# Expert loop of a two-layer mixture model: down products ahead of the next gate and up, and the pair's sum in two parts

## The chip, the cores and the metric

The kernel runs on one core of one Trainium2 chip. The metric is the device time of one execution in microseconds. Times of the program before come from three runs; the profile is one more execution, recorded by the hardware profiler.

## The reference

A block of two layers on 256 tokens of width 1024, all in float32. Layer 0 mixes tokens by attention, layer 1 by pooled means. After each mixer every token goes to two of 32 experts (inner width 512):

```python
h2 = modulate(rms_norm(x, norm2_g[i]), sh2, s2)
experts, gates = route(h2, router_w, router_b)        # two experts and two gates for each token
...
def expert_block(args):
    xb, e = args
    return (jax.nn.silu(xb @ w_gate[e]) * (xb @ w_up[e])) @ w_down[e]
...
x = x + g2 * out                                      # out: gated sum over a token's two experts
```

## The kernel before

Five engine programs are written by hand and meet at counting semaphores; there is no scheduler. What matters here is `experts(L)`, which each of the engines has once for layer `L`, and the loads on SP.

*Tokens into slots.* Every expert has 64 slots. The tokens are gathered into `dense` (columns by slot) by products with a selection matrix on TensorE, in two halves of 256 slots; each half has eight steps k (L814, L819), and ScalarE and VectorE evict them with the modulation (L1180, L1749). GpSimd copies the 64 slots of expert e into one of two buffers `xw` (L465).

*One expert.* TensorE computes gate and up in two halves of four steps k each (`gate_up`, L825, 16 profiled matmul records a half) into PSUM bank 4. ScalarE applies silu (L1205), VectorE multiplies by up (L1773) and counts `h_ready`. TensorE transposes the hidden values (two, L835) into bank 5, ScalarE copies them to `t_sb` (L1199) and counts `t_ready`. TensorE computes the down product into bank 6 (`down`, L844) and counts `dn_done`. VectorE multiplies it by the layer's output gate into `y_sb`, in two column halves f (`gated_outputs`, L1755), and counts `y_v`, two for each expert.

*Two experts make a pair*, with 128 rows in `y_sb`. The pair's selection `sg` (VectorE's `choose`, L1740 and L1744) is transposed too (L833), and `combine` (L853) adds the rows back to the tokens in PSUM banks 0 to 3: two products for each half f. In the loop, e is the expert and c its place in a body of six; the second expert of a pair has c odd. Before the loop TensorE has done expert 0 whole and gate and up of expert 1.

*Weights.* The ring has three slots of one expert each. SP loads expert e in its queue's order: gate and up of the first half (2 DMAs of 1 MB) when TensorE has counted `gu_half` for expert e - 3, of the second half when it has counted `gu_done`, and down (2 MB) when it has counted `dn_done`. The landings are counted by `gu_in`, `gu2_in` and `dn_in`. Experts 0, 1 and 2 are loaded ahead of the layer's loop. Behind expert 31 of layer 0 the same queue loads the pool mixer's weights.

## Time and profile before

| | |
|---|---|
| three runs | 1310.32, 1314.6, 1315.19 us; median 1314.6 |
| profiled execution | 1308.68 us, span 1306.9 us |
| TensorE busy | 1200.5 us, 92% of the span |
| VectorE, ScalarE, GpSimd busy | 458.7, 178.4, 73.4 us |
| HBM read | 484.00 MB, 371 GB/s over the span |
| TensorE's granted clock | 0.982 of full speed |

The expert loops take some two thirds of the span: about 314 to 756 us for layer 0 and 860 to 1302 us for layer 1. A busy share is a mean over stages: which resource ends a stage last must be read inside it. In the rows further down PE is TensorE, ACT ScalarE, DVE VectorE, POOL GpSimd, and SPq a DMA issue on SP's queue.

### The profile page before, as it was taken

To read this page: it belongs to the slowest core of one execution; us is meant where nothing else is said; L and a number is where in the kernel's file an instruction comes from. 1 tells how busy PE (TensorE), PEld (TensorE's weight loads), DVE (VectorE), ACT (ScalarE), POOL (GpSimd) and SP (SyncE) were. 2 spreads that over 40 slices of the span, in tenths; PEclk is the share of its full clock that TensorE was granted. 3 is DMA by queue.
4 is the path that set the end of the run, shared out by engine and by line. 5 is a ranking of instruction groups with operands and counts; after the bars stand their busy time and mean duration, and the time that the engine had idled before them with its cause. 6 is when DMAs were issued, how large, how long until landed. Compare 5 with 4: busy or idle time off the path is not lost.

```text
span 1306.9 us, 13664 instructions
## 1 busy us (share of the span) xinstructions
PE 1200.5 (92%) x5008; PEld 492.8 (38%) x5008; DVE 458.7 (35%) x933; ACT 178.4 (14%) x375; POOL 73.4 (6%) x86
## 2 busy tenths in 40 slices
PE   6999999889999999898998899899999998988897
PEld 3444445544333333232332376443333332322232
DVE  4296676577122212121121156642222221211112
ACT  2212126522000000000000021310000000000000
POOL 0113100000000000000000000000000000000000
PEclk9999999999999999899998999999999998999999
DMA  9948759286999999999999997589999999999995
GB/s 355 399 184 347 261 205 401 97 346 251 410 422 421 422 423 422 421 422 422 422 422 423 418 406 297 222 329 415 422 422 422 422 421 422 422 422 422 422 422 235
DMA packets 80933, 485.50 MB, mean 371 GB/s; under 512 B 6146, under 2 KB 7682, under 8 KB 31748
## 3 DMA queue, kind: packets, MB, share of 16 engines
q1 hardware_dynamic: 79168, 481.91, 90.3%
q10 hardware_dynamic: 1732, 3.16, 0.7%
q8 instruction: 20, 0.33, 0.1%
q14 instruction: 13, 0.11, 0.0%
HBM read 484.00 MB, written 1.05 MB: 371 GB/s over the span
## 4 chain that ended last, share of the span: by engine, by line
PE 57%; SPq 18%; DMA 15%; DVE 4%; issue 3%; ACT 3%; POOL 0%; DVEq 0%; ACTq 0%
PE PS L825 19%; SPq L325 14%; DMA ring<-in_moe_w_up 13%; PE PS L844 10%; PE PS L635 8%; PE PS L853 4%; SPq L330 3%; PE PS L605 2%; PE PS L707 2%; PE PS L997 2%; PE PS L972 2%; DMA ring<-in_attn_w_in 2%; PE PS L835 1%; DVE KQH L1773 1%; ACT ring L1071 1%
## 5 line engine op out<-in xcount | busy, mean ns | idle before, releaser
L825 PE MATMUL PS<-ring,KQH 128*64 128x512 f32 x2048 | 480.5, 613 | 30.1 <-DMA ring<-in_moe_w_up 28.6
L825 PEld LDWEIGHTS PS<-ring,KQH 128*64 128x64 f32 x2048 | 146.1, 141 | 311.0 <-issue 277.0
L844 PE MATMUL PS<-ring,KQH 128*64 128x512 f32 x1024 | 230.8, 592 | 2.3 <-ACT KQH L1191 1.4
L844 PEld LDWEIGHTS PS<-ring,KQH 128*64 128x64 f32 x1024 | 73.0, 137 | 147.8 <-issue 144.6
L1755 DVE TENSOR_TENSOR TMP<-PS,KQH 64x512 f32<-64x512 f32 x64 | 44.1, 689 | 228.8 <-PE PS L844 227.8
L1755 DVE TENSOR_TENSOR TMP<-PS,TMP 64x512 f32<-64x512 f32 x64 | 44.1, 689 | 227.8 <-PE PS L844 226.7
L853 PE MATMUL PS<-TMP,KQH 128*128 128x512 f32 x256 | 118.4, 605 | 1.6 <-DVE TMP L1755 1.6
L1205 ACT ACTIVATE KQH<-PS 128x256 f32<-128x256 f32 x62 | 23.8, 384 | 665.5 <-PE PS L825 646.0
L635 PE MATMUL PS<-ring,KQH 128*128 128x512 f32 x256 | 114.0, 593 | 0.0
L1773 DVE TENSOR_TENSOR KQH<-KQH,PS 128x256 f32<-128x256 f32 x64 | 38.7, 605 | 157.3 <-ACT KQH L1205 157.3
L465 POOL COPY KQH<-KQH 128x512 f32 x62 | 38.1, 617 | 831.5 <-PE PS L825 771.2
L853 PEld LDWEIGHTS PS<-TMP,KQH 128*128 128x128 f32 x256 | 46.0, 189 | 73.6 <-issue 70.3
L635 PEld LDWEIGHTS PS<-ring,KQH 128*128 128x128 f32 x256 | 46.5, 190 | 54.0 <-issue 54.0
L1740 DVE TENSOR_SCALAR rope_g<-const,route 128x128 f32<-128x128 f32 x128 | 35.7, 342 | 76.1 <-PE PS L835 75.7
L835 PE MATMUL PS<-const,KQH 128*128 128x128 f32 x128 | 26.2, 287 | 34.0 <-DVE KQH L1773 34.0
L448 POOL TENSOR_TENSOR stat<-stat,mhalf 128x16 f32<-128x16 f32 (+3 forms) x18 | 35.0, 1942 | 361.3 <-DVE stat L1546 130.8
L1366 DVE SCALAR_TENSOR_TENSOR ring<-ring,ccols 128x1024 f32<-128x1024 f32 x42 | 54.0, 1285 | 3.3 <-DMA ring<-in_ada_w 1.8
L1199 ACT COPY KQH<-PS 128x256 f32<-128x256 f32 (+1 forms) x62 | 29.5, 476 | 147.4 <-PE PS L835 147.4
L835 PEld LDWEIGHTS PS<-const,KQH 128*128 128x128 f32 x128 | 14.4, 140 | 61.4 <-DVE KQH L1773 61.4
L605 PE MATMUL PS<-ring,KQH 128*128 128x512 f32 x64 | 29.4, 619 | 1.8 <-DMA ring<-in_attn_w_in 1.8
L707 PE MATMUL PS<-ring,KQH 128*128 128x512 f32 x64 | 28.0, 594 | 0.9 <-ACT KQH L1078 0.9
L972 PE MATMUL PS<-KQH,ring 128*128 128x257 f32 x128 | 28.2, 379 | 0.0
(249 smaller groups left out, 788.0 us busy)
## 6 DMA issues: line engine op xcount, KB each, us to landing
ring<-in_moe_w_gate SPq DMA_DIRECT2D x128, 1024.0 KB, 26.5
ring<-in_moe_w_up SPq DMA_DIRECT2D x128, 1024.0 KB, 26.6
ring<-in_moe_w_down SPq DMA_DIRECT2D x64, 2048.0 KB, 27.9
ring<-in_ada_w SPq DMA_DIRECT2D x23, 2048.0 KB, 13.3
ring<-in_attn_w_in SPq DMA_DIRECT2D x2, 4096.0 KB, 12.7
ring<-in_attn_w_in SPq DMA_DIRECT2D x2, 2048.0 KB, 21.0
ring<-in_attn_w_out SPq DMA_DIRECT2D x1, 4096.0 KB, 24.1
ring<-in_pool_w_in SPq DMA_DIRECT2D x1, 4096.0 KB, 27.9
```

Source lines behind the costliest of these rows:

```text
L325: sp.dma_start(gu_w[s][:, a, 4 * part:4 * part + 4, :], w[L.l, e].rearrange("(p k) f -> p k f", p=P)[:, 4 * part:4 * part + 4, :]).then_in ...
L605: ins = mm(bank(4 + 2 * n + half), hT[:, k, P * n:P * n + P], unit(2)[:, k, 512 * half:512 * half + 512], start=k == 0, stop=k == KC - 1)
L635: ins = mm(bank(4 + 2 * (n % 2) + half), hT[:, k, P * t:P * t + P], unit(u)[:, k, 512 * half:512 * half + 512], start=k == 0, stop=k == KC ...
L707: ins = mm(bank(4 + q), oT[:, h, P * (q // 2):P * (q // 2) + P], unit(2)[:, h, 512 * (q % 2):512 * (q % 2) + 512], start=h == 0, stop=h == ...
L825: ins = mm(PS[64 * f:64 * f + 64, 4, :], xs[:, k, 0:SLOTS], gu_w[s][:, :, k, 256 * f:256 * f + 256], start=k == 0, stop=k == KC - 1)
L835: ins = tr(PS[:, 5, 256 + P * c:256 + P * c + P], h_sb[:, P * c:P * c + P], ident)
L844: ins = mm(PS[64 * f:64 * f + 64, 6, :], lhs, dn_w[s][:, c, 512 * f:512 * f + 512], start=c == 0, stop=c == 3)
L853: ins = mm(bank(2 * t + f), t_sb[:, P * t:P * t + P], y_sb[:, 512 * f:512 * f + 512], start=False, stop=done is not None, skip_group_check ...
L972: ins = mm(PS[:, n % 4, 0:SEQ + 1], pool_w[:, k, P * b:P * b + P], xa[:, k, :], start=k == 0, stop=k == KC - 1)
L1366: ins = V.scalar_tensor_tensor(acc, unit(u)[:, k, :], ccols[:, 32 * k:32 * k + 1], acc, ALU.mult, ALU.add)
L1755: return V.tensor_tensor(y_sb[64 * second:64 * second + 64, 512 * f:512 * f + 512], PS[64 * f:64 * f + 64, 6, :], g[64 * f:64 * f + 64, 51 ...
L1773: V.tensor_tensor(h_pairs, silu_sb.rearrange("p (q b) -> p q b", b=2), PS[:, 4, 256:512].rearrange("p (q b) -> p q b", b=2), ALU.mult).the ...
```

## The change

It reorders TensorE's program and adapts ScalarE and VectorE to it.

- TensorE does, for each expert, transposes, down product, then gate and up of the next expert, both halves in a row. Before, down stood between the two halves.
- The sum of a pair (experts e - 1 and e, c odd) is split: its first column half comes behind gate and up of expert e + 1, the second behind gate and up of expert e + 2. Between them lie transposes and down of e + 1.
- The selection is transposed with the pair's second expert (c odd), before with its first.
- VectorE writes the second gated half of a pair's first expert only when TensorE has done the transposes of the next expert (`tr_done`), since the sum before reads these columns until then.
- At the layer's start, expert 0's transposes of the hidden values move between the gathers of k = 3 and 4 of the second half, with a copy of 256 columns instead of 512. The selection's transposes leave this place.
- The last pair of a layer is summed at once, as before.

```diff
--- before.py
+++ after.py
@@ -845,15 +845,55 @@
                                  start=c == 0, stop=c == 3)
                 return ins
 
-            def combine(L, y, done=None):
-
-                for f in range(2):
-                    pe.wait_ge(L.y_v, y + f + 1)
-                    for t in range(NT):
-                        ins = mm(bank(2 * t + f), t_sb[:, P * t:P * t + P], y_sb[:, 512 * f:512 * f + 512], start=False,
-                                 stop=done is not None, skip_group_check=True)
-                        if done is not None:
-                            ins.then_inc(done, 1)
+            def combine(L, y, f, done=None):
+
+                pe.wait_ge(L.y_v, y + f + 1)
+                for t in range(NT):
+                    ins = mm(bank(2 * t + f), t_sb[:, P * t:P * t + P], y_sb[:, 512 * f:512 * f + 512], start=False,
+                             stop=done is not None, skip_group_check=True)
+                    if done is not None:
+                        ins.then_inc(done, 1)
+
+            def second_places(L, k):
+
+                for t in range(NT):
+                    gather_high(1, k, t)
+                    ins = gather_low(1, k, t)
+                ins.then_inc(L.xg_done, 1)
+
+            def turn_hidden(L, e, c, it):
+
+                pe.wait_ge(L.h_ready, e + 1)
+                if c % 2:
+                    pe.wait_ge(L.sg_ready, 3 * it + (c // 2 + 1))
+                transposes(sg if c % 2 else None).then_inc(L.tr_done, 1)
+
+            def gate_up_first(L, e, c, it):
+
+                pe.wait_ge(L.gu_in[L.slot(c)], (2 * it + c // 3) * 32 + 32)
+                pe.wait_ge(L.xw_ready, e)
+                gate_up(L.slot(c), xw[c % 2], range(4)).then_inc(L.gu_half, 1)
+
+            def gate_up_second(L, e, c, it):
+
+                pe.wait_ge(L.gu2_in[L.slot(c)], (2 * it + c // 3) * 32 + 32)
+                gate_up(L.slot(c), xw[c % 2], range(4, KC)).then_inc(L.gu_done, 1)
+
+            def down_product(L, e, c, it):
+
+                pe.wait_ge(L.t_ready, e + 1)
+                pe.wait_ge(L.dn_in[L.slot(c)], (2 * it + c // 3) * 16 + 16)
+                pe.wait_ge(L.y_v, 2 * e)
+                down(L.slot(c)).then_inc(L.dn_done, 1)
+
+            def sum_and_next(L, e, c, it):
+
+                combine(L, 2 * e, 0)
+                turn_hidden(L, e + 1, c + 1, it)
+                down_product(L, e + 1, c + 1, it)
+                gate_up_first(L, e + 2, c + 2, it)
+                gate_up_second(L, e + 2, c + 2, it)
+                combine(L, 2 * e, 1)
 
             def combine_overflow():
 
@@ -887,57 +927,41 @@
                 pe.wait_ge(L.gu2_in[L.slot(0)], 32)
                 gate_up(L.slot(0), dense, range(4, KC)).then_inc(L.gu_done, 1)
                 pe.wait_ge(L.picked, 4)
-                for k in range(KC):
+                for k in range(4):
                     if k == 3:
                         pe.wait_ge(L.slots_known, 1)
-                    if k >= 4:
-                        pe.wait_ge((L.xs_v, L.xs_a)[k % 2], 4 + (k - 4) // 2 + 1)
-                    for t in range(NT):
-                        gather_high(1, k, t)
-                        ins = gather_low(1, k, t)
-                    ins.then_inc(L.xg_done, 1)
+                    second_places(L, k)
                 pe.wait_ge(L.h_ready, 1)
-                pe.wait_ge(L.sg_ready, 1)
-                transposes(sg).then_inc(L.tr_done, 1)
+                transposes(None).then_inc(L.tr_done, 1)
+                for k in range(4, KC):
+                    pe.wait_ge((L.xs_v, L.xs_a)[k % 2], k // 2 + 3)
+                    second_places(L, k)
                 pe.wait_ge(L.t_ready, 1)
                 pe.wait_ge(L.xs_v, 7)
                 pe.wait_ge(L.dn_in[L.slot(0)], 16)
                 down(L.slot(0)).then_inc(L.dn_done, 1)
-                pe.wait_ge(L.gu_in[L.slot(1)], 32)
-                pe.wait_ge(L.xw_ready, 1)
-                gate_up(L.slot(1), xw[1], range(4)).then_inc(L.gu_half, 1)
-                pe.wait_ge(L.gu2_in[L.slot(1)], 32)
-                gate_up(L.slot(1), xw[1], range(4, KC)).then_inc(L.gu_done, 1)
+                gate_up_first(L, 1, 1, 0)
+                gate_up_second(L, 1, 1, 0)
                 pe.wait_ge(L.xs_a, 8)
                 pe.wait_ge(mod_used, TURN[LATE[L.l]] + 1)
                 add_zero(False)
 
-                def step(e, c, it, last=False):
-
-                    n = c + 1
-                    pe.wait_ge(L.h_ready, e + 1)
-                    if c % 2 == 0:
-                        pe.wait_ge(L.sg_ready, 3 * it + (c // 2 + 1))
-                    transposes(None if c % 2 else sg).then_inc(L.tr_done, 1)
-                    if not last:
-                        pe.wait_ge(L.gu_in[L.slot(n)], (2 * it + n // 3) * 32 + 32)
-                        pe.wait_ge(L.xw_ready, e + 1)
-                        gate_up(L.slot(n), xw[n % 2], range(4)).then_inc(L.gu_half, 1)
-                    pe.wait_ge(L.t_ready, e + 1)
-                    pe.wait_ge(L.dn_in[L.slot(c)], (2 * it + c // 3) * 16 + 16)
-                    if c % 2:
-                        pe.wait_ge(L.y_v, 2 * e)
-                    down(L.slot(c)).then_inc(L.dn_done, 1)
-                    if not last:
-                        pe.wait_ge(L.gu2_in[L.slot(n)], (2 * it + n // 3) * 32 + 32)
-                        gate_up(L.slot(n), xw[n % 2], range(4, KC)).then_inc(L.gu_done, 1)
-                    if c % 2:
-                        combine(L, 2 * e, L.acc_done if last else None)
+
+                def pair(e, c, it):
+
+                    turn_hidden(L, e, c, it)
+                    down_product(L, e, c, it)
+                    gate_up_first(L, e + 1, c + 1, it)
+                    gate_up_second(L, e + 1, c + 1, it)
+                    sum_and_next(L, e, c, it)
 
                 with pe.Fori(0, TURNS) as it:
-                    for c in range(1, BODY + 1):
-                        step(BODY * it + c, c, it)
-                step(BODY * TURNS + 1, 1, TURNS, last=True)
+                    for c in range(1, BODY + 1, 2):
+                        pair(BODY * it + c, c, it)
+                turn_hidden(L, NE - 1, 1, TURNS)
+                down_product(L, NE - 1, 1, TURNS)
+                for f in range(2):
+                    combine(L, 2 * NE - 2, f, L.acc_done)
 
 
                 n_ov = pe.value_load(ov_info[0:1, OVER:OVER + 1], min_val=0, max_val=OVER)
@@ -1188,14 +1212,14 @@
                 spread(L, 1, 1)
                 spread(L, 1, 3)
                 act.wait_ge(L.tr_done, 1)
-                nc.scalar.copy(t_sb, PS[:, 5, :]).then_inc(L.t_ready, 1)
+                nc.scalar.copy(t_sb[:, 256:512], PS[:, 5, 256:512]).then_inc(L.t_ready, 1)
                 for k in range(5, KC, 2):
                     spread(L, 1, k)
 
                 def step(e, c, last=False, first=False):
                     if not first:
                         act.wait_ge(L.tr_done, e + 1)
-                        a = 256 * (c % 2)
+                        a = 256 * (1 - c % 2)
                         nc.scalar.copy(t_sb[:, a:512], PS[:, 5, a:512]).then_inc(L.t_ready, 1)
                     else:
                         act.wait_ge(routed, L.l + 1)
@@ -1782,24 +1806,28 @@
                 V.memset(HT[:, 0:SLOTS], 0.0).then_inc(L.xs_v, 1)
                 dve.wait_ge(L.xs_v, 9)
                 mod_use(LATE[L.l])
+                dve.wait_ge(mod_used, TURN[LATE[L.l]] + 1)
 
                 def step(e, c, it, last=False):
-                    if c % 2 == 0 and not isinstance(it, int):
+                    if c % 2 and not last:
                         V.tensor_scalar(pcur, pcur, -float(PAIR), None, ALU.add).then_inc(L.chosen, 1)
                         g = 3 * it + c // 2
                         dve.wait_ge(L.chosen, 2 * g + 2)
                         dve.wait_ge(L.tr_done, e + 1)
                         choose(PAIR, sg, L.chosen, 2 * g + 3, L.sg_ready)
                     dve.wait_ge(L.dn_done, e + 1)
-                    for f in range(2):
-                        gated_outputs(L, c % 2, f).then_inc(L.y_v, 1)
-                    if not last:
+                    gated_outputs(L, c % 2, 0).then_inc(L.y_v, 1)
+                    if c % 2 == 0:
                         hidden(e + 2)
-
+                        dve.wait_ge(L.tr_done, e + 2)
+                    gated_outputs(L, c % 2, 1).then_inc(L.y_v, 1)
+                    if c % 2 and not last:
+                        hidden(e + 2)
+
+                step(0, 0, 0)
                 with dve.Fori(0, TURNS) as it:
-                    for c in range(BODY):
+                    for c in range(1, BODY + 1):
                         step(BODY * it + c, c, it)
-                step(BODY * TURNS, 0, TURNS)
                 step(BODY * TURNS + 1, 1, TURNS, last=True)
 
                 link(V.tensor_scalar(pcur, pos, -float(NE * SLOTS - SLOTS), None, ALU.add))
```

The first place is TensorE's at the layer's start, from the last gather product of the second half to expert 1's gate and up. Names in brackets are the semaphores waited for. Before:

```order
L814 MATMUL PS<-PICK,HI 128x256 [waits xs_a0]
L819 MATMUL PS<-PICK,LO 128x256
L814 MATMUL PS<-PICK,HI 128x256
L819 MATMUL PS<-PICK,LO 128x256
L833 MATMUL PS<-const,KQH 128x128 [waits sg_ready0,h_ready0]
L833 MATMUL PS<-const,KQH 128x128
L835 MATMUL PS<-const,KQH 128x128 x2
L844 MATMUL PS<-ring,KQH 64x512 [waits dn_in0_0,xs_v0,t_ready0]
L844 MATMUL PS<-ring,KQH 64x512 x7
```

In the changed kernel, the gathers of k = 3 (last two products) and the first of k = 4:

```order
L814 MATMUL PS<-PICK,HI 128x256
L819 MATMUL PS<-PICK,LO 128x256
L835 MATMUL PS<-const,KQH 128x128 [waits h_ready0]
L835 MATMUL PS<-const,KQH 128x128
L814 MATMUL PS<-PICK,HI 128x256 [waits xs_v0]
L819 MATMUL PS<-PICK,LO 128x256
L814 MATMUL PS<-PICK,HI 128x256
L819 MATMUL PS<-PICK,LO 128x256
```

and from k = 7 on:

```order
L814 MATMUL PS<-PICK,HI 128x256 [waits xs_a0]
L819 MATMUL PS<-PICK,LO 128x256
L814 MATMUL PS<-PICK,HI 128x256
L819 MATMUL PS<-PICK,LO 128x256
L844 MATMUL PS<-ring,KQH 64x512 [waits dn_in0_0,xs_v0,t_ready0]
L844 MATMUL PS<-ring,KQH 64x512 x7
L825 MATMUL PS<-ring,KQH 64x512 [waits xw_ready0,gu_in0_1]
```

The transposes of the selection (L833) are gone from here, those of the hidden values (L835) stand four gather steps earlier, and nothing is left between the last gather and down (L844).

The second place is TensorE's first expert of the loop, c = 1. Rows L825 are gate and up (x8 is a half), L844 down, L853 (L852 in the changed kernel) the sum; ISA and REGISTER_ALU rows hold waits. Before:

```order
L835 MATMUL PS<-const,KQH 128x128 x2
L923 ISA
L825 MATMUL PS<-ring,KQH 64x512 x8
L927 ISA
L929 ISA
L844 MATMUL PS<-ring,KQH 64x512 x8
L825 MATMUL PS<-ring,KQH 64x512 x8
L851 REGISTER_ALU
L853 MATMUL PS<-TMP,KQH 128x512 x2
L851 REGISTER_ALU
L853 MATMUL PS<-TMP,KQH 128x512 x2
```

In the changed kernel, up to the first expert of the next pair:

```order
L868 ISA
L833 MATMUL PS<-const,KQH 128x128 x2
L835 MATMUL PS<-const,KQH 128x128 x2
L885 ISA
L886 ISA
L844 MATMUL PS<-ring,KQH 64x512 x8
L873 ISA
L825 MATMUL PS<-ring,KQH 64x512 x16
L850 REGISTER_ALU
L852 MATMUL PS<-TMP,KQH 128x512 x2
L866 REGISTER_ALU
L835 MATMUL PS<-const,KQH 128x128 x2
```

Down has moved ahead of both halves of gate and up, four transposes stand directly ahead of it, and only half of the sum stands ahead of the next transposes.

The third place is VectorE's loop from the outputs of a pair's one expert to those of the next. L1755 (L1779 in the changed kernel) is one gated column half, L1773 (L1797) the hidden product, L1788 (L1813) the first step of choosing the next selection. Before, from a pair's first expert on:

```order
L1755 TENSOR_TENSOR TMP<-PS,TMP 64x512 [waits dn_done0]
L1755 TENSOR_TENSOR TMP<-PS,TMP 64x512
L1772 REGISTER_ALU
L1773 TENSOR_TENSOR KQH<-KQH,PS 128x128x2 [waits silu_done0]
L1755 TENSOR_TENSOR TMP<-PS,TMP 64x512 [waits dn_done0]
L1755 TENSOR_TENSOR TMP<-PS,TMP 64x512
L1772 REGISTER_ALU
L1773 TENSOR_TENSOR KQH<-KQH,PS 128x128x2 [waits silu_done0]
L1788 TENSOR_SCALAR route<-route 128x4
```

In the changed kernel, from a pair's second expert on:

```order
L1779 TENSOR_TENSOR TMP<-PS,TMP 64x512 [waits dn_done0]
L1779 TENSOR_TENSOR TMP<-PS,TMP 64x512
L1796 REGISTER_ALU
L1797 TENSOR_TENSOR KQH<-KQH,PS 128x128x2 [waits silu_done0]
L1779 TENSOR_TENSOR TMP<-PS,TMP 64x512 [waits dn_done0]
L1796 REGISTER_ALU
L1797 TENSOR_TENSOR KQH<-KQH,PS 128x128x2 [waits silu_done0]
L1779 TENSOR_TENSOR TMP<-PS,TMP 64x512 [waits tr_done0]
L1813 TENSOR_SCALAR route<-route 128x4
```

The second gated half of a pair's first expert has moved behind the hidden product and waits for TensorE's transposes.

## Rows read from the trace of the kernel before

**Rows 1.** Page, part 4: the chain that ended last, shares of the span by engine

```profile
PE 57%; SPq 18%; DMA 15%; DVE 4%; issue 3%; ACT 3%; POOL 0%; DVEq 0%; ACTq 0%
```

**Rows 2.** The chain in order of time: start us, length us, what

```profile
330.69 3.43 PE PS L844 x16
...
337.55 3.63 PE PS L853 x8
...
364.08 3.63 PE PS L853 x8
...
709.25 26.67 DMA ring<-in_moe_w_up
```

**Rows 3.** Stretches: us, busy time (instructions) by engine, granted clock, DMA share, GB/s

```profile
321.00:322.00 1.00, 1.00 (x8) 0.39 (x6) 0.00 (x0) 0.00 (x0) 0.00 (x0) 1.00 0.92 385
...
335.00:336.00 1.00, 1.00 (x6) 0.29 (x4) 0.58 (x1) 0.00 (x0) 0.00 (x0) 1.00 1.33 262
336.00:337.00 1.00, 1.00 (x8) 0.29 (x4) 0.00 (x0) 0.00 (x0) 0.00 (x0) 1.00 0.54 197
...
880.00:881.00 1.00, 1.00 (x8) 0.35 (x6) 0.81 (x2) 0.00 (x0) 0.00 (x0) 1.00 1.11 311
881.00:882.00 1.00, 1.00 (x8) 0.37 (x6) 0.00 (x0) 0.00 (x0) 0.00 (x0) 1.00 0.53 156
...
540.00:740.00 200.00, 180.17 (x740) 61.69 (x742) 37.34 (x75) 11.33 (x26) 7.41 (x12) 0.95 1.01 422
```

**Rows 4.** Timeline, SP's queue: start us, us, engine, line, out and in

```profile
318.67 0.38 SPq L330 DMA_DIRECT2D ring<-in_moe_w_down  x1
...
334.16 0.38 SPq L330 DMA_DIRECT2D ring<-in_moe_w_down  x1
...
713.91 2.14 SPq L325 DMA_DIRECT2D ring<-in_moe_w_up  x1
```

**Rows 5.** Timeline at layer 0's start: start us, us, engine, line, [idle before, releaser]

```profile
313.58 0.28 PE L819 MATMUL PS<-PICK,LO 128*128 128x256 f32 x1
...
314.33 0.59 ACT L1191 COPY KQH<-PS 128x512 f32<-128x512 f32 x1 [1.79 <-PE PS L835]
...
314.97 3.65 PE L844 MATMUL PS<-ring,KQH 128*64 128x512 f32 x16 [0.68 <-ACT KQH L1191]
...
316.34 1.17 POOL L465 COPY KQH<-KQH 128x512 f32 x2 [30.14 <-DVE KQH L1782]
...
326.66 0.44 PE L835 MATMUL PS<-const,KQH 128*128 128x128 f32 x2 [0.20 <-DVE KQH L1773]
327.03 3.65 PE L825 MATMUL PS<-ring,KQH 128*64 128x512 f32 x16
```

**Rows 6.** Timeline at the end of layer 0's loop, experts 30 and 31

```profile
735.05 0.38 PE L833 MATMUL PS<-const,KQH 128*128 128x128 f32 x2
...
735.68 0.59 ACT L1199 COPY KQH<-PS 128x512 f32<-128x512 f32 x1 [3.67 <-PE PS L835]
...
743.10 1.41 DVE L1755 TENSOR_TENSOR TMP<-PS,TMP 64x512 f32<-64x512 f32 x2 [10.45 <-PE PS L844]
...
747.60 0.44 PE L835 MATMUL PS<-const,KQH 128*128 128x128 f32 x2 [1.12 <-DVE KQH L1773]
...
748.50 3.65 PE L844 MATMUL PS<-ring,KQH 128*64 128x512 f32 x16 [0.46 <-ACT KQH L1199]
```

**Rows 7.** DMA issues at 713.91 us, expert 31's second part: size, us to landing

```profile
ring<-in_moe_w_up SPq DMA_DIRECT2D x1, 1024.0 KB, 27.0
```

**Rows 8.** Timeline at the end of layer 1's loop, TensorE

```profile
1282.24 3.65 PE L825 MATMUL PS<-ring,KQH 128*64 128x512 f32 x16 [0.32 <-DMA ring<-in_moe_w_up]
...
1294.77 3.65 PE L844 MATMUL PS<-ring,KQH 128*64 128x512 f32 x16 [0.46 <-ACT KQH L1199]
```

**Rows 9.** Timeline in layer 0's loop, TensorE, two halves of gate and up

```profile
661.43 3.65 PE L825 MATMUL PS<-ring,KQH 128*64 128x512 f32 x16 [1.53 <-DMA ring<-in_moe_w_up]
...
691.25 6.56 PE L825 MATMUL PS<-ring,KQH 128*64 128x512 f32 x16 [2.84 <-DMA ring<-in_moe_w_up]
```

## The prediction

> **What bounds the kernel now.** I read the page first, then the chain of work that ended last, then the expert loop in slices, the start and end of a layer's loop in order of time, and the DMA issues with their landings. The chain gives TensorE 57%, but 18% lies in SP's queue and 15% in a DMA [rows 1], so two resources take turns. The expert loop begins bound by TensorE: it enters with three experts loaded, and the chain runs through TensorE alone, a pair of experts from sum to sum taking 364.08 - 337.55 = 26.53 us [rows 2]. One expert's weights are 6,144 KB; at the 422 GB/s of [rows 3] they take 14.9 us, a pair 29.8. So the lead shrinks by 3.3 us a pair until TensorE waits for weights. From then on the loop is bound by the DMA: in 540 to 740 us the DMA engines are full and TensorE is idle for 20 of 200 us [rows 3]. The whole loop therefore ends when the stream of weights ends, plus what TensorE has left to do behind it. Three things can move that: idle time of the stream, which exists only at the layer's start; the work behind the last weights; and a TensorE that becomes slower than 14.9 us per expert.
>
> **Head, first hole in the stream.** SP issues expert 3's down weights when the first down product is done; they go out at 318.67 us [rows 4], and the stream, empty by then, is back at 385 GB/s in the slice from 321 us [rows 3]. Before: the last gather product starts at 313.58, then four transposes, ScalarE's copy of 128x512 at 314.33, and the down product at 314.97, 1.39 us behind the gather [rows 5]. The change puts expert 0's two transposes of the hidden values between the gathers of k = 3 and 4, and leaves those of the selection to expert 1. The two cost the gathers about 0.36 us (at 326.66 and 327.03 a gate and up half starts 0.37 us after the first of two transposes [rows 5]), and the copy, now 128x256, runs beside the gathers that are left. So down starts at 313.58 + 0.12 + 0.36 = 314.06, which is 0.9 us earlier. What stands next: expert 1's gate and up need GpSimd's window. Its two copies took 1.17 us from 316.34 [rows 5], the first is half of that; VectorE's work ahead of them moves 0.36 us later with the gathers, so the window is there at 316.34 + 0.36 + 0.59 = 317.3, and down ends at 314.06 + 3.43 = 317.5. Hidden, by 0.2 us. The stream restarts 0.9 us earlier: **-0.9 per layer**.
>
> **Head, second hole.** Before, expert 1's down product stands behind half of expert 2's gate and up; expert 4's down weights are issued at 334.16, and the stream moves only 262 and 197 GB/s in the slices from 335 and 336 us, short by (844 - 459)/422 = 0.9 us of transfer [rows 3, 4]. In the change expert 1 does transposes, down, gate and up. The transposes start 0.9 us before 326.66, down behind them by 1.40 us (worked out below) at 327.16, and it ends at 330.6: SP can issue 3.5 us earlier. An issue takes about 2.3 us to bring the stream back (318.67 to 321), so it flowed again at 336.5, and with 0.9 us lost it had run dry at about 335.6; in the change that is 334.7. 330.6 + 2.3 = 332.9 lies 1.8 us ahead of it, so the hole closes: **-0.9** in layer 0. Layer 1 shows it too: 311 and 156 GB/s, (844 - 467)/422 = 0.9 us [rows 3]. The next issues keep ahead: two parts of 2 MB (5.0 us of transfer each) go out at about 334 and 338, the next down weights at about 344, when the queue holds work to 349.
>
> **Middle of the loop.** The cost of the new order is exposed latency. Down now stands directly behind its transposes. For an even expert (two transposes, copy of 256 columns) the row with nothing between is the layer's last: 747.60 to 748.50, 0.90 us [rows 6]. For an odd expert (four transposes) ScalarE's copy starts 0.63 us after the first transpose and takes 0.59 (735.05 and 735.68); but down also waits for VectorE's second gated half, which in the change waits for the same transposes: 0.63 + 0.70 (half of 1.41) + 0.07 = 1.40 us [rows 6]. Against that the wait for silu and the hidden product of 1.12 us in each pair goes, since half a sum (3.63/2 = 1.8 us [rows 2]) now stands over it each time. A pair by these terms: 1.40 + 0.90 + two downs 6.86 + four halves of gate and up 2 x (3.5 + 3.43) + two half sums 3.6 = 26.6, against 26.53. **0 in the TensorE-bound part**, and no matter: the stream is full there.
>
> In the DMA-bound part let T be the landing of an expert's first gate and up (709.25 + 26.67 = 735.92 for expert 31 [rows 2]). The second halves land 5.0 us later, at 713.91 + 27.0 = 740.9 [rows 4, 7]. TensorE does the first half to T + 3.5, waits 1.5, and from T + 5.0 does second half, half sum, transposes, down: 3.43 + 1.8 + 1.40 + 3.43, to T + 15.1. The next expert lands at T + 14.9 and its second half at T + 19.9, so 0.2 us late costs nothing: **0**. The order before hid the 5.0 us between the landings under a down product; the new one does not, but spends slack of 14.9 - 13.3 = 1.6 us per expert.
>
> **Tail.** Before: T = 735.92, first half, down of expert 30, second half, silu, hidden, transposes, copy; down of 31 starts at 748.50, T + 12.6 [rows 6]. In layer 1 the same, 1282.24 to 1294.77 [rows 8]. In the change down of 30 is done before T. Second half from T + 5.0 to T + 8.4, second half of the sum to T + 10.2 (silu and hidden, the 1.12 us of idle before 747.60, lie under it), transposes and copy 1.40: down of 31 starts at T + 11.65. Its weights are there: 2 MB behind T + 5.0, T + 10. What follows is the same in both. **-0.9 per layer**.
>
> **Sum.** 2 x (0.9 + 0.9 + 0.9) = 5.4 us. In layer 0 the gain passes through the pool section, whose chain is TensorE products and the norm behind the last sum; its weights come on the stream and move by 1.8 of the 2.7, which I take as enough. The profiled execution took 1308.7 us (span 1306.9): 1303.3. It lies 5.9 us under the median of the three runs, so against the median 1314.6 - 5.4 = 1309.2, or -0.41%. A measurement of this kernel tells about 0.5%, 6.6 us, from no change; the forecast lies inside that.
>
> **The clock, where the trace and a rule are weighed.** Rows at either level: the gate and up half behind 2.84 us of waiting took 6.56 us, behind 1.53 us of waiting 3.65 [rows 9]; the granted clock of 540 to 740 us is 0.95 [rows 3], so some stretches stand at 1.2 GHz and most at 2.4. The change splits the waits into 1.5 us ahead of each second half and about 1 us ahead of each down, all nearer to the second row, so I take the full clock. The Trainium skill (TensorE: Matmul & The Clock Gate, HAM oscillation) says that a wait for a DMA at every tile can send each burst behind it back to half rate, even if the work itself is enough; by that rule this order, which waits twice per expert, is a danger, and rival B gives its price.
>
> **Rivals.**
> A. *Only part of the gain:* the holes close but the stream is not the bound at the end (or the reverse). Either half alone: -3.6 for the head, -1.8 for the tail: 1311.0 or 1312.8. For it: the cover of GpSimd's window is only 0.2 us. Against: the landings at the tail fit the waits to 0.1 us.
> B. *Slower, by the clock:* each second half runs at the lower clock. The price is up to 6.56 - 3.65 = 2.9 us per expert; TensorE then needs 13.3 + 2.9 = 16.2 against 14.9, 1.3 too much over the some 14 experts of a layer that wait: 2 x 14 x 1.3 = 36, less the 5.4: 1345. It decides from 1.6 us per expert on; below, the slack takes it. Against: no wait of 1.5 us did it.
> C. *The clock at the tail alone:* the last second half runs low in both layers, 2 x 2.9 = 5.8 back: 1315.0, no change. It is the one place in the loop where no slack takes the loss.
> D. *More:* the wait ahead of the last down is shorter than 1.40. Its floor is the landing at T + 10, 1.65 us less per layer: -5.4 - 3.3 = -8.7, 1305.9. For it: VectorE and ScalarE work at the same time. Against: both durations are in rows.
>
> **How the numbers follow.** Forecast 0.55, A 0.13, B 0.05, C 0.10, D 0.17. The forecast, A and C end within 0.5%; D and the part of the forecast's scatter that falls under -6.6 (the three runs spread over 4.9 us) make faster 0.30; B and a scatter upward make slower 0.07; same 0.63. The range runs from D's 1305.9, less 1.4 for the spread, to C's 1315.0: 1304.5 to 1315. B is left out.
>
> **What would show each step.** Down of expert 0 starts 0.5 us behind the last gather, not 1.39; SP issues expert 3's down weights at about 317.8; no slice under 390 GB/s near 335 and 880; pairs at the start of the loop 26.4 to 26.7 us; waits of about 1.5 us ahead of every second gate and up half, at full clock; last down 11.7 us behind the landing of expert 31's first part. Wrong if the granted clock of 540 to 740 us falls well under 0.95, if TensorE stops waiting for weights there, or if the stream has new holes.

## The result, and the profile after

The changed kernel took 1302.72 us (median of 4 runs, 1301.58 to 1303.26) against 1313.18 for the kernel before in the same comparison (4 runs, 1310.32 to 1315.19): ratio 0.9923, 95% interval [0.9908, 0.9938]. Two later comparisons gave 0.9929 and 0.9935. By the means of the runs the three comparisons give 10.4, 8.9 and 8.1 us. So it is 0.7 to 0.8% faster, 8 to 10 us, where 5.4 were forecast, and 1302.72 lies below the stated range of 1304.5 to 1315. The profiled execution took 1301.58 us, its span is 1299.7 (1308.68 and 1306.9 before).

The chain that ended last, by engine, in the changed kernel's profile page:

```profile
PE 56%; SPq 29%; DMA 5%; DVE 4%; ACT 3%; issue 2%; POOL 0%; DVEq 0%; ACTq 0%; POOLq 0%
```

TensorE's share stands almost where it was (57%), but the waits for a landing DMA fell from 15% to 5% and SP's queue, which carries the stream of weights, rose from 18% to 29% [rows 1]: the stream of weights bounds more of the chain, and TensorE stands still for it less.

The start of layer 0's loop on TensorE in order of time:

```profile
310.22 0.41 PE L835 MATMUL PS<-const,KQH 128*128 128x128 f32 x2
...
312.25 0.28 PE L819 MATMUL PS<-PICK,LO 128*128 128x256 f32 x1
312.46 3.65 PE L844 MATMUL PS<-ring,KQH 128*64 128x512 f32 x16
315.95 7.04 PE L825 MATMUL PS<-ring,KQH 128*64 128x512 f32 x32
...
325.76 3.65 PE L844 MATMUL PS<-ring,KQH 128*64 128x512 f32 x16 [0.87 <-DVE TMP L1779]
```

and on SP the two issues of down weights:

```profile
316.16 0.38 SPq L330 DMA_DIRECT2D ring<-in_moe_w_down  x1
...
329.45 0.38 SPq L330 DMA_DIRECT2D ring<-in_moe_w_down  x1
```

Expert 0's transposes (310.22) now stand between the gathers, and its down product starts at 312.46, right behind the last one [rows 5 had 1.39 us]. Expert 1's gate and up follows at 315.95 without a wait, so GpSimd's window was there. This execution came to the layer's first gate and up at 301.19 us, the one of before at 302.75. Counted from there, the first down product stands at 11.27 us where it stood at 12.22, and the two issues at 14.97 and 28.26 where they stood at 15.92 and 31.41 [rows 4].

The stretches of [rows 3] in the changed kernel (PE, weight load, DVE, ACT and POOL busy; granted clock, DMA share, GB/s):

```profile
317.00:318.00 1.00, 1.00 (x6) 0.29 (x4) 0.00 (x0) 0.00 (x0) 0.00 (x0) 1.00 1.05 147
...
335.00:336.00 1.00, 1.00 (x6) 0.15 (x2) 0.00 (x0) 0.00 (x0) 0.00 (x0) 1.00 0.96 401
336.00:337.00 1.00, 1.00 (x4) 0.49 (x3) 0.26 (x1) 0.38 (x1) 0.00 (x0) 1.00 1.00 418
...
540.00:740.00 200.00, 178.59 (x762) 59.96 (x761) 39.16 (x83) 11.68 (x27) 7.37 (x12) 1.00 1.01 422
880.00:881.00 1.00, 1.00 (x5) 0.39 (x3) 0.08 (x1) 0.00 (x0) 0.45 (x1) 1.00 1.05 434
881.00:882.00 1.00, 0.46 (x4) 0.20 (x4) 0.00 (x0) 0.37 (x1) 0.00 (x0) 1.00 1.02 426
```

The first hole is still there (317 us), but smaller: the transfer missing in it is 1.3 us where it was 2.2. The slices near 335 and 880 us are full; the second hole has gone in both layers. Longer stretches show each hole whole. Layer 0's first and second, then layer 1's, in the kernel before:

```profile
312.00:326.00 14.00, 13.32 (x71) 5.71 (x70) 7.22 (x21) 2.44 (x5) 1.17 (x2) 1.00 0.89 357
326.00:360.00 34.00, 32.68 (x145) 11.29 (x144) 6.49 (x13) 2.10 (x5) 1.85 (x3) 1.00 1.01 411
854.00:872.00 18.00, 17.12 (x95) 8.19 (x92) 10.25 (x27) 3.41 (x7) 1.58 (x3) 1.00 0.92 369
872.00:920.00 48.00, 46.88 (x204) 16.61 (x206) 9.80 (x21) 3.07 (x7) 2.06 (x4) 1.00 1.00 409
```

and in the changed kernel:

```profile
312.00:326.00 14.00, 12.69 (x62) 4.65 (x63) 5.87 (x16) 1.71 (x4) 1.78 (x3) 1.00 0.97 385
326.00:360.00 34.00, 32.61 (x144) 11.46 (x142) 8.57 (x19) 1.72 (x4) 1.23 (x2) 1.00 1.01 421
854.00:872.00 18.00, 16.70 (x84) 6.44 (x85) 7.82 (x21) 2.10 (x4) 1.78 (x3) 1.00 0.97 393
872.00:920.00 48.00, 46.07 (x200) 16.21 (x197) 8.76 (x17) 2.86 (x7) 1.91 (x4) 1.00 1.01 421
```

Against a full stream of 422 GB/s the kernel before misses 2.2 us of transfer in the first hole of either layer and 0.9 and 1.5 us in the second; the changed kernel misses 1.2 us in the first and 0.1 us in the second. In 540 to 740 us the DMA engines move the same 422 GB/s, and the granted clock is 1.00 where it was 0.95.

The end of layer 0's loop and of layer 1's, TensorE:

```profile
732.57 3.65 PE L825 MATMUL PS<-ring,KQH 128*64 128x512 f32 x16
737.53 3.65 PE L825 MATMUL PS<-ring,KQH 128*64 128x512 f32 x16 [1.31 <-DMA ring<-in_moe_w_up]
741.12 1.98 PE L852 MATMUL PS<-TMP,KQH 128*128 128x512 f32 x4
742.94 0.38 PE L833 MATMUL PS<-const,KQH 128*128 128x128 f32 x2
743.16 0.38 PE L835 MATMUL PS<-const,KQH 128*128 128x128 f32 x2
744.42 3.65 PE L844 MATMUL PS<-ring,KQH 128*64 128x512 f32 x16 [0.88 <-DVE TMP L1779]
...
1280.70 3.65 PE L825 MATMUL PS<-ring,KQH 128*64 128x512 f32 x16 [1.33 <-DMA ring<-in_moe_w_up]
...
1287.58 3.65 PE L844 MATMUL PS<-ring,KQH 128*64 128x512 f32 x16 [0.88 <-DVE TMP L1779]
```

The first part of expert 31's gate and up landed at 732.50 (its issue plus its time to landing) and is used at 732.57; down of 31, at 744.42, follows that landing by 11.92 us, as it does in layer 1 (12.58 and 12.59 before [rows 2, 6, 8]). The second half of the sum (741.12) now covers silu and the hidden product, and the second gate and up half waits 1.3 us and still takes 3.65 us.

**Where the time came from.** I took four profiled executions with the code before (the first, before_again, before_third, and warm_head_before, which was the same in time) and five of the change (the first, after_again, after_third, after_fourth, warm_head_after), and cut each at the same events. "Landing" is the issue of expert 31's first part plus its time to landing. Mean us:

| stretch | before | change | difference | forecast |
|---|---|---|---|---|
| start to layer 0's first gate and up | 303.2 | 302.7 | -0.5 | 0 |
| from there to landing of expert 31's first part, layer 0 + layer 1 | 434.0 + 433.9 | 431.5 + 431.4 | -5.0 | -3.6 |
| landing to expert 31's down, layer 0 + layer 1 | 12.8 + 13.6 | 11.9 + 11.9 | -2.6 | -1.8 |
| the rest (down to end of the sum, pool section, end) | | | 0.0 | 0 |
| span | 1309.2 | 1301.1 | -8.1 | -5.4 |

The second row varies by itself: 433.2 to 435.0 us in the eight layers before, 431.1 to 431.7 in the ten of the change.

### The profile page after: what moved, and what is told of

Read it like the earlier page. It is cut to its first block, busy times and chain, and to the rows that moved or that the text cites. A ratio compares the mean times of both kernels' runs of the same rounds, so it can differ in the third digit from the quotient of the medians.

```text
span 1299.7 us, 13694 instructions
## 1 busy us (share of the span) xinstructions
PE 1191.6 (92%) x5006; PEld 491.7 (38%) x5008; DVE 453.3 (35%) x933; ACT 178.3 (14%) x375; POOL 73.2 (6%) x86
## 4 chain that ended last, share of the span: by engine, by line
PE 56%; SPq 29%; DMA 5%; DVE 4%; ACT 3%; issue 2%; POOL 0%; DVEq 0%; ACTq 0%; POOLq 0%
SPq L325 24%; PE PS L825 18%; PE PS L844 9%; PE PS L635 8%; SPq L330 5%; PE PS L852 4%; DMA ring<-in_moe_w_up 4%; PE PS L707 2%; PE PS L605 2%; PE PS L1021 2%; PE PS L996 2%; DVE TMP L1779 1%; PE PS L814 1%; PE PS L578 1%; PE PS L819 1%
## 5 line engine op out<-in xcount | busy, mean ns | idle before, releaser
L825 PE MATMUL PS<-ring,KQH 128*64 128x512 f32 x2048 | 456.0, 594 | 25.0 <-DMA ring<-in_moe_w_up 23.4
L844 PE MATMUL PS<-ring,KQH 128*64 128x512 f32 x1024 | 233.8, 598 | 44.0 <-DVE TMP L1779 26.8
L825 PEld LDWEIGHTS PS<-ring,KQH 128*64 128x64 f32 x2048 | 147.7, 137 | 322.0 <-issue 267.7
L1797 DVE TENSOR_TENSOR KQH<-KQH,PS 128x256 f32<-128x256 f32 x64 | 38.9, 608 | 417.1 <-ACT KQH L1229 417.1
L844 PEld LDWEIGHTS PS<-ring,KQH 128*64 128x64 f32 x1024 | 70.0, 136 | 166.5 <-issue 132.0
L852 PE MATMUL PS<-TMP,KQH 128*128 128x512 f32 x256 | 126.4, 617 | 1.6 <-DVE TMP L1779 1.6
L635 PE MATMUL PS<-ring,KQH 128*128 128x512 f32 x256 | 114.0, 593 | 0.0
L1779 DVE TENSOR_TENSOR TMP<-PS,KQH 64x512 f32<-64x512 f32 x64 | 44.1, 689 | 134.5 <-PE PS L844 113.2
L1779 DVE TENSOR_TENSOR TMP<-PS,TMP 64x512 f32<-64x512 f32 x64 | 44.1, 689 | 134.4 <-PE PS L844 113.2
L852 PEld LDWEIGHTS PS<-TMP,KQH 128*128 128x128 f32 x256 | 43.5, 189 | 83.6 <-issue 80.3
L1223 ACT COPY KQH<-PS 128x512 f32<-128x512 f32 (+1 forms) x62 | 29.9, 482 | 114.0 <-PE PS L835 114.0
L605 PE MATMUL PS<-ring,KQH 128*128 128x512 f32 x64 | 27.9, 593 | 1.8 <-DVE KQH L1417 1.8
L707 PE MATMUL PS<-ring,KQH 128*128 128x512 f32 x64 | 28.0, 593 | 0.9 <-ACT KQH L1102 0.9
L1021 PE MATMUL PS<-ring,KQH 128*128 128x512 f32 x64 | 27.6, 592 | 0.0
L996 PEld LDWEIGHTS PS<-KQH,ring 128*128 128x128 f32 x128 | 24.1, 189 | 3.5
```

Source lines behind the costliest of these rows:

```text
L605: ins = mm(bank(4 + 2 * n + half), hT[:, k, P * n:P * n + P], unit(2)[:, k, 512 * half:512 * half + 512], start=k == 0, stop=k == KC - 1)
L635: ins = mm(bank(4 + 2 * (n % 2) + half), hT[:, k, P * t:P * t + P], unit(u)[:, k, 512 * half:512 * half + 512], start=k == 0, stop=k == KC ...
L707: ins = mm(bank(4 + q), oT[:, h, P * (q // 2):P * (q // 2) + P], unit(2)[:, h, 512 * (q % 2):512 * (q % 2) + 512], start=h == 0, stop=h == ...
L825: ins = mm(PS[64 * f:64 * f + 64, 4, :], xs[:, k, 0:SLOTS], gu_w[s][:, :, k, 256 * f:256 * f + 256], start=k == 0, stop=k == KC - 1)
L844: ins = mm(PS[64 * f:64 * f + 64, 6, :], lhs, dn_w[s][:, c, 512 * f:512 * f + 512], start=c == 0, stop=c == 3)
L852: ins = mm(bank(2 * t + f), t_sb[:, P * t:P * t + P], y_sb[:, 512 * f:512 * f + 512], start=False, stop=done is not None, skip_group_check ...
```

## The experiments

Each has its median and its ratio to the kernel before in the same comparison. "Mean" is the mean of its timed runs; that of the kernel before was 1312.4 in the first three comparisons of this section and 1311.9 in the last. I held three theories. **H** (the prediction's): holes and tail, nothing else. **K**: the lower clock, which the kernel before falls into behind its long waits, costs it more than the forecast's zero, and the change ends that. **E** (late): the difference ahead of the loops belongs to the change, too. The recorded expectations call H theory 1 and K theory 2, and call theory F that this difference is not the change's.

### The kernels again, and each part alone

before_again: the kernel before, unchanged.

> The kernel before once more, unchanged, to see what its executions differ in. Theory 1 (the whole gain is the two holes in the stream of weights and the shorter tail, 5.4 us; the rest of the measured 10.5 us is where the executions of the kernel before happened to fall): some executions come near the profiled 1308.7 us, the ratio is 1.000, and the spread is a shift of the stages ahead of the expert loops. Theory 2 (in the kernel before TensorE's clock falls in its long waits for weights, and in most executions this costs time at a place without slack): executions gather near 1313 us, and in a profile of such a one a stretch at the lower clock stands in the tail of a layer or in the stages behind it, worth 3 to 6 us.

1311.99 us, 0.9999 [0.9984, 1.0013]. Its profile was 2.6 us longer than the first one. At the end of layer 0, TensorE:

```profile
719.66 0.44 PE L835 MATMUL PS<-const,KQH 128*128 128x128 f32 x2 [1.13 <-DVE KQH L1773]
...
722.92 5.03 PE L825 MATMUL PS<-ring,KQH 128*64 128x512 f32 x16 [2.82 <-DMA ring<-in_moe_w_up]
727.78 3.60 PE L844 MATMUL PS<-ring,KQH 128*64 128x512 f32 x16
...
738.82 3.65 PE L825 MATMUL PS<-ring,KQH 128*64 128x512 f32 x16
...
751.35 3.65 PE L844 MATMUL PS<-ring,KQH 128*64 128x512 f32 x16 [0.46 <-ACT KQH L1199]
```

The half at 722.92 is expert 30's first. It stands behind 2.82 us of waiting and takes 5.03 instead of 3.65 us; from there to expert 31's half at 738.82 TensorE waits for nothing, so it has become the late one, and down of 31 (751.35) follows its landing by 13.6 us, where 12.6 is the value without lateness.

after_again: the changed kernel again.

> The changed kernel once more beside the others. Theory 1: executions spread as those before do, ratio between 0.993 and 0.997. Theory 2: ratio 0.992 again, a spread of under 2 us, granted clock 0.997.

1303.44 us, 0.9929 [0.9909, 0.9948].

head_only: the changed start of the layer, with the order of the loop and the whole sum as before (and the selection's transposes at odd steps). In excerpt, against the changed kernel; VectorE, too, writes both gated halves together again:

```
+    def step(e, c, it):
+        turn_hidden(L, e, c, it)
+        gate_up_first(L, e + 1, c + 1, it)
+        down_product(L, e, c, it)
+        gate_up_second(L, e + 1, c + 1, it)
+        if c % 2:
+            for f in range(2):
+                combine(L, 2 * e, f)
     ...
-        pair(BODY * it + c, c, it)
+        step(BODY * it + c, c, it)
```

> The head of the change alone (expert 0's transposes between the gathers, the selection transposed with the pair's second expert); in the loop down stands between the halves of gate and up and the sum is whole, as before. Theory 1: the first hole of 0.9 us per layer closes by 0.9, the second by about 0.9 too (all of the loop's start is 0.9 earlier but the hole itself stays, so only the shift counts): -1.8 us in all, ratio 0.9985. Theory 2: the same small gain, and the executions spread as those of the kernel before do, near 1311 us, with a mean granted clock of about 0.98.

1310.40 us, 0.9984 [0.9972, 0.9996]: -1.9 us by the means, 0.5 to 3.7 by the interval. The head's term of 1.8 fits; the interval is too wide to confirm its size.

loop_only: the changed kernel with expert 0's transposes behind all gathers again (in excerpt).

```
-    transposes(None).then_inc(L.tr_done, 1)
     for k in range(4, KC):
         ...
+    transposes(None).then_inc(L.tr_done, 1)
```

> The change with expert 0's transposes behind all gathers again; loop order and split sum as in the change. Theory 1: loses 0.6 to 0.9 us per layer against the change: about 4 us under the kernel before, ratio 0.997. Theory 2: granted clock 0.997, executions near 1304.5 us, 8 to 9 us under the kernel before, ratio 0.9935.

1303.82 us, 0.9934 [0.9914, 0.9954]. Its down product of expert 0 starts 0.5 us later than the change's, behind a wait of 0.46 us for ScalarE's copy. Its mean is 0.7 us above that of after_again, less than these runs can tell from nothing: nearly the whole gain stays with the loop's part.

split_only: the changed kernel with each down product back between the halves of gate and up (in excerpt; the same in `pair`).

```
     turn_hidden(L, e + 1, c + 1, it)
-    down_product(L, e + 1, c + 1, it)
     gate_up_first(L, e + 2, c + 2, it)
+    down_product(L, e + 1, c + 1, it)
     gate_up_second(L, e + 2, c + 2, it)
```

> The change with down back between the halves of gate and up; head and split sum stay. Both theories: the head gives 1.9 us; the second hole stays open (down of expert 1 is again behind half of a gate and up); the nominal tail is 13.5 us behind the landing, 1 us per layer longer than in the kernel before, since the second half of the sum and the selection's transposes stand ahead of the last down. Theory 1: 1312 us, ratio 1.000. Theory 2: the waits for weights are spread evenly over the experts, the clock stays up, the lateness at the last expert is gone: about 1309 us, ratio 0.9975, granted clock 0.997.

1310.63 us, 0.9988 [0.9975, 1.0000]. H expected 1.000; K expected 0.9975 with a clock that stays up, but the granted clock of the program was 0.978. The sum is split, but TensorE waits 2.0 to 2.3 us for weights again, and the lower clock is back; layer 0 near its end:

```profile
722.23 5.35 PE L825 MATMUL PS<-ring,KQH 128*64 128x512 f32 x16 [2.05 <-DMA ring<-in_moe_w_up]
```

down_only: the changed kernel with the sum in one piece behind the next expert's gate and up, down first everywhere (in excerpt; VectorE writes both gated halves together again).

```
-    combine(L, 2 * e, 0)
+    for f in range(2):
+        combine(L, 2 * e, f)
     turn_hidden(L, e + 1, c + 1, it)
     down_product(L, e + 1, c + 1, it)
     ...
-    combine(L, 2 * e, 1)
```

> The change with the pair's sum whole behind the next gate and up; head and the place of down stay. At the last expert no half sum stands between gate and up and the transposes: 5.0 + 3.4 + 1.15 (silu, hidden) + 1.3 = 10.9 us from landing to the last down, 1.0 us per layer less than in the change, if TensorE is on time. Behind a pair's second expert TensorE is 1.4 us late for the next weights and catches up at the second half. Theory 1: 1301.5 us, ratio 0.9915. Theory 2: the same where the clock stays up; if the waits are uneven enough to let it fall, 1303 to 1306 and a wider spread.

1333.61 us, 1.0165 [1.0143, 1.0187]: 22 us slower. No theory had this. TensorE in the middle of layer 0:

```profile
589.28 5.35 PE L844 MATMUL PS<-ring,KQH 128*64 128x512 f32 x16 [0.86 <-ACT KQH L1223]
...
617.60 0.43 PE L833 MATMUL PS<-const,KQH 128*128 128x128 f32 x2 [1.19 <-DVE KQH L1797]
617.87 0.38 PE L835 MATMUL PS<-const,KQH 128*128 128x128 f32 x2
619.10 3.65 PE L844 MATMUL PS<-ring,KQH 128*64 128x512 f32 x16 [0.85 <-ACT KQH L1223]
```

At odd experts nothing covers silu and hidden (1.19 us), and the copy behind the transposes adds 0.85. Behind these two waits, with only the four transposes between, the down product takes 5.35 us at some experts (589.28) and 3.65 at others (619.10): slow in 8 of the 16 pairs of layer 0 and in 7 of those of layer 1, about every second one. 15 times 1.7 us is 25 us. And no half in either layer waits for weights: TensorE enters the loop behind the stream (which has three experts landed), needs 14.4 us per expert here (from 316.0 to 762.89 for 31), the stream 14.9, and so gains 0.5 us per expert, too little to catch up within the layer. Down of 31 comes 26.6 us behind its landing in layer 0 and 26.7 in layer 1, in place of 11.9. The changed kernel needs 13.5 us per expert while nothing is awaited (325.76 to 406.55 for six), and its first wait for weights is here:

```profile
603.37 3.65 PE L825 MATMUL PS<-ring,KQH 128*64 128x512 f32 x16 [0.97 <-DMA ring<-in_moe_w_up]
```

### The clock in the loops

keep_warm: the kernel before with a filler product of 128x512 on each side of the transposes at odd steps (bank 7, whose content nothing reads; in excerpt).

```
+    if c % 2 and not last: stay_busy(1, 7)
     pe.wait_ge(L.h_ready, e + 1)
     ...
     transposes(None if c % 2 else sg).then_inc(L.tr_done, 1)
+    if c % 2 and not last: stay_busy(1, 7)
```

> The kernel before, with two filler products (128x512 float32 into a PSUM bank that nobody reads) in the step of each pair's second expert, one ahead of the transposes and one behind them, where TensorE otherwise waits 1.1 us for the hidden product and up to 2.8 us for weights. They add 1.7 us of TensorE's work to a pair, which has 3.3 us of slack against the stream. Theory 1 (only the holes and the nominal tail count, the rest is scatter of other stages): no change, 1312 us, ratio 1.000. Theory 2 (the clock falls in the waits, TensorE then reaches the last expert late in some executions): granted clock of the 540 to 740 us stretch 1.00, the spread falls from 8 us to 2 or 3, median about 1309, ratio 0.9975, and the last down starts 12.6 us behind the landing of expert 31 in both layers.

1311.05 us, 0.9991 [0.9979, 1.0003]. The granted clock of the program rose to 0.994 (0.982 before), and down of 31 follows its landing by 12.6 us in both layers, as K expects, but the gain is under half of the 3 us that K expected. The fillers also delay the start of the loop: in 326 to 360 us the stream moves 392 GB/s where it moved 411, so the second hole of layer 0 grew from 0.9 to 2.4 us.

keep_warm_late: the same at c = 3 and 5 only, so that the loop's first step is clean.

> The kernel before with the two filler products only in two of three pairs (experts 3 and 5 of each body of six), so not where the stream has its second hole. Theory 2 (TensorE, at the lower clock behind long waits, reaches the last expert late): the stream's holes are those of the kernel before (2.2 and 1.1 us per layer), the last downs start 12.6 us behind the landing, and the time is 2.5 to 3 us under the kernel before, 1309.3, ratio 0.998, with a spread of under 5 us. Theory 1 (scatter of other stages): ratio 1.000.

1311.51 us, 0.9991 [0.9980, 1.0002]; mean 1311.25, -1.1, and the standard deviation of its runs is 1.2 us where the kernel before had 1.9 in that comparison. Its down of 31 follows the landing by 12.55 and 12.61 us.

down_only_warm: down_only with one filler product in the uncovered wait (in excerpt, against down_only).

```
     for c in range(1, BODY + 1, 2):
+        if c > 1: stay_busy(1, 7)
         pair(BODY * it + c, c, it)
+    stay_busy(1, 7)
```

> The kernel with down ahead and the sum whole (it took 1333.6 us) plus one filler product (0.86 us) in the wait for the hidden product where no half sum stands. It adds no time to that wait of 1.1 us. If the 21 us over the kernel before were the lower clock behind this gap, they go: granted clock 0.997, about 1302 us, ratio 0.992. If they were the exposed latencies themselves, nothing changes: 1333 us or more, ratio 1.0165.

1308.96 us, 0.9973 [0.9960, 0.9986]: a product that does nothing takes 25 us off down_only, as much as the 15 slow down products cost there. It did not reach the expected 0.992. The same place of the loop:

```profile
549.63 1.13 PE L755 MATMUL PS<-const 128*128 128x512 f32 x2
550.89 0.43 PE L833 MATMUL PS<-const,KQH 128*128 128x128 f32 x2
551.16 0.38 PE L835 MATMUL PS<-const,KQH 128*128 128x128 f32 x2
552.30 3.65 PE L844 MATMUL PS<-ring,KQH 128*64 128x512 f32 x16 [0.76 <-ACT KQH L1226]
```

The filler (one product, two instructions, at 549.63) stands in the 1.19 us, no down product of either layer is slow any more, and the granted clock of 540 to 740 us is 1.00 (0.97 in down_only). TensorE needs 14.07 us per expert ((721.16 - 552.30) / 12), so it gains 0.8 us per expert on the stream and is almost there at the end: down of 31 at 14.9 and 15.0 us behind its landing, 3.0 later than in the change in each layer. That is 6.0 us. The mean lies at 1308.6, against 1302.7 for the one execution of the change in this comparison and 1303.5 and 1303.8 for its means in two others: 4.8 to 5.9.

### The tail, and the start of the program

short_tail: the changed kernel with the last pair of each layer written out; the second half of the last sum and the last selection's transposes stand between the halves of expert 31's gate and up (in excerpt; VectorE's wait for the transposes goes there too).

```
     gate_up_first(L, e + 2, c + 2, it)
+    combine(L, 2 * e, 1)
+    pe.wait_ge(L.sg_ready, 3 * TURNS + 1)
+    for t in range(NT):
+        tr(PS[:, 5, P * t:P * t + P], sg[:, t, :], ident)
     gate_up_second(L, e + 2, c + 2, it)
-    combine(L, 2 * e, 1)
     ...
+    transposes(None).then_inc(L.tr_done, 1)
```

> The change, with the last pair of each layer written out: the second half of the sum of experts 28 and 29 and the last selection's transposes stand between the two halves of gate and up of expert 31, in TensorE's wait of 1.3 us for weights; VectorE writes the gated half behind the hidden product without the wait for transposes. From the landing: 3.5 + 1.8 + 0.4 + 3.4 (second half) + 1.1 (silu, hidden) + 1.1 (transposes, copy) = 11.2 against 11.9 us, so -0.7 per layer, -1.4 in all, against the change: ratio 0.9915 to the kernel before. If the exposed wait of 1.1 us lets the clock fall there, the last down takes 5.4 instead of 3.5 us and the gain is gone.

1302.51 us, 0.9930 [0.9915, 0.9945]. Down of 31 follows its landing by 11.65 instead of 11.9 us: the sum no longer covers the 1.12 us of silu and hidden. The expected 0.7 us per layer did not come, and 0.25 is less than a comparison of this kernel can tell.

before_third and after_third are one profiled execution each, with 1313.65 and 1302.68 us.

> The kernel before once more, one look at its stages. Theory 1: last downs at 12.6 us behind the landing of expert 31 in both layers. Theory 2: in at least one layer more than that, 13 to 15 us, with the last gate and up half at the lower clock one or two experts ahead of it.

> The changed kernel once more, one look: the stages ahead of the first expert loop are the same code as in the kernel before. If their length (301.2 to 304.7 us so far to the first gate and up) is chance alone, it should come near 304.4 in some execution of the changed kernel too. The loops: holes of 1.3 us and none, last downs 11.9 us behind the landing.

In before_third's profile, and in six of the fourteen up to here, part of the stretch near 26 us stood at 1.2 GHz (granted clock 0.72 over 25 to 31 us) and TensorE came to the first expert at 304.3 to 304.7 us, where the others came at 301.2 to 303.0; after_third was one of the others (302.8), and none of the six was the changed kernel, loop_only or short_tail. The code there is the same in all. To test theory E, two fillers went into TensorE's wait of 1.8 us ahead of that place, in the kernel before (warm_head_before), in the changed one (warm_head_after) and in keep_warm_late (warm_both_before):

```
+    for _ in range(2): mm(bank(7), ones, const[:, 0:512], start=True, stop=True)
     first_keys(0)
```

> The kernel before with two filler products of 128x512 (0.86 us each, into a bank that the next product overwrites) in TensorE's wait of 1.8 us ahead of the first key projection, at 23.4 us. In 6 of 14 profiles (before_again, before_third, head_only, split_only, down_only, keep_warm_late) the clock stood at 1.2 GHz from 26.0 to 29 us, behind this wait, and the first expert's gate and up came at 304.3 to 304.7 us; in the other 8 it did not and they came at 301.2 to 303.0. Theory E (that fall is a part of the gain that was missed: the kernel before has it in some executions): without it the mean falls by 0.8 to 1.7 us against the kernel before of the same call, and the profile has the clock at 1.00 from 26 to 29 us and the first gate and up at 302 to 303. Theory F (it comes and goes with something else, or the stream of weights hides it): within 0.5 us of before, ratio 0.9997 to 1.0003.

> The changed kernel with the same two filler products at 23.4 us. Theory E: the changed kernel's three profiles did not show the fall at 26 us, so nothing is won: within 0.4 us of after_fourth in this call, and the distance to warm_head_before is 7 to 8 us where that of after to before was 8.9. Theory F: the distance stays at 8.5 to 9.3 us, both kernels moving alike.

> The kernel before with the two fillers at 23.4 us and those of keep_warm_late around the transposes of steps 3 and 5 of each turn. If both effects of the clock are real and add up, its mean lies 1.9 to 2.9 us below the kernel before of the call (1.1 from the loops, 0.8 to 1.7 from the head), ratio 0.9978 to 0.9985, with a standard deviation near 1 us; what then still parts it from after, 6 to 7 us, is what the prediction's three terms measured in the profiles (5.9 to 6.2). If only the loops' part is real: ratio 0.9991 as keep_warm_late had.

> The changed kernel again, as the mate of the three above on this chip: 1302.6 to 1304.0 us, ratio 0.9920 to 0.9940, the clock at 1.00 at 26 us in its profile, the first gate and up at 301.2 to 303.0 us (theory E). If this profile shows the fall at 26 us too, it isn't tied to the kernel.

| | median | mean | ratio to before |
|---|---|---|---|
| warm_head_before | 1311.68 | 1311.9 | 1.0001 [0.9991, 1.0011] |
| warm_head_after | 1302.79 | 1302.7 | 0.9930 [0.9915, 0.9944] |
| warm_both_before | 1309.68 | 1309.5 | 0.9980 [0.9969, 0.9991] |
| after_fourth | 1304.33 | 1303.8 | 0.9935 [0.9920, 0.9950] |

The stretch from 25 to 31 us (TensorE busy, granted clock, DMA share, GB/s) in before_again, in after_fourth and in warm_head_before:

```profile
25.00:31.00 6.00, 5.81 (x10) 0.72 1.04 392
```

```profile
25.00:31.00 6.00, 5.59 (x9) 0.72 1.04 394
```

```profile
25.00:31.00 6.00, 5.91 (x15) 1.00 1.04 392
```

The unchanged code fell to the lower clock in the changed kernel as well (after_fourth), and with the fall prevented the kernel before is not faster. Theory E falls: the distance between the two warmed kernels is 9.2 us by the means, no smaller than without the fillers (8.1). What the stretch ahead of the loops added to the difference of single profiles is chance. (after_fourth itself had 1304.33, above the 1302.6 to 1304.0 that were expected.) The same profile of warm_head_before shows theory K at its plainest, at the end of layer 1:

```profile
1266.20 6.61 PE L827 MATMUL PS<-ring,KQH 128*64 128x512 f32 x16 [2.83 <-DMA ring<-in_moe_w_up]
1272.63 3.60 PE L846 MATMUL PS<-ring,KQH 128*64 128x512 f32 x16
1276.07 3.60 PE L827 MATMUL PS<-ring,KQH 128*64 128x512 f32 x16
...
1283.66 3.65 PE L827 MATMUL PS<-ring,KQH 128*64 128x512 f32 x16
...
1296.20 3.65 PE L846 MATMUL PS<-ring,KQH 128*64 128x512 f32 x16 [0.46 <-ACT KQH L1201]
```

Behind 2.83 us of waiting the half takes 6.61 us. Expert 31's half, due 14.9 us after 1266.20 at 1281.1, starts at 1283.66 with no wait, and the down product is 15.15 us behind the landing, 2.6 more than the 12.6 of [rows 8].

warm_both_before gave -2.3 us by the means, where keep_warm_late alone gave -1.1. The intervals of the two overlap (0.9969 to 0.9991, 0.9980 to 1.0002), and the head's fillers alone gave nothing, so I read the three kernels with fillers in the loop (0.9991, 0.9991, 0.9980) as one effect. Each of the first two intervals includes no change; my estimate from the three together, by their means and standard deviations, is 1.6 us, with a 95% interval of 0.9 to 2.2. What the lower clock costs the kernel before is real, and small. The fillers at steps 3 and 5 did not end it: in warm_both_before's profile TensorE still takes 5.35 us behind a wait of 1.96 us (721.85), and down of 31 in layer 0 comes 13.9 us behind its landing.

## Why the prediction came out as it did

**Direction: right. Mechanism: right for the change, one term missing for the kernel before.** The stream was the bound, its holes and the tail moved, and the new order cost nothing in the middle.

**Head, first hole: right in kind.** The down product starts 0.95 us earlier against 0.9 predicted, and GpSimd's window is hidden. The missing transfer 10 to 20 us behind the layer's first gate and up fell from 2.2 to 1.3 us in the mean of the four and five profiles, in both layers. head_only, which has this term alone, won 1.9 us for two layers against 1.8 (interval 0.5 to 3.7). loop_only, with the transposes back behind the gathers, was 0.7 us longer than after_again.

**Head, second hole: right in kind, too small.** It closes in both layers. The missing transfer from 30 to 50 us behind the first gate and up is 1.3 us in the mean of the eight layers before (1.2 in layer 0, 1.5 in layer 1) and nothing in the change. I priced 0.9 and took it from two slices in each layer; the slices beside them and a third dip (near 351 us in layer 0) were left out, and in layer 1 these hold a third of the loss. So both holes together are worth 2.2 us per layer, where 1.8 were forecast. From first gate and up to expert 31's landing the mean gain is 2.5 per layer: a term of 3.6 for both layers, measured 5.0, of which 4.4 are seen as holes. The other 0.6 is not located; it is less than the scatter of that stretch (up to 1.8 us between layers of the kernel before).

**Middle and tail: the step that failed is the clock.** "I take the full clock" held for the changed kernel, whose clock is 1.00 in 540 to 740 us: rivals B and C did not come. It was wrong for the kernel before, and so was the term of 0 for the clock at the last expert. I had its granted clock of 0.95 and a half of 6.56 us among my rows [rows 3, 9] and used them only to ask what the change might lose. That the kernel before was paying for it, and that the change would end it, I never priced; rival C names the one place without slack, but only as a loss of the change. In the four profiles of the code before, expert 31's down came 0.0 to 2.6 us later than at the full clock, 0.65 in the mean of eight layers; that is 1.3 us of the gain where the forecast had 0. It was late in three of the eight, by 1.0, 1.3 and 2.6 us, and in just these three TensorE had waited 2.8 us ahead of expert 30's first half, which then took 5.03 to 6.61 us; in the other five it had waited 0.3 to 1.6 us there, and the half took 3.65. The fillers in the loop took 1.6 us (0.9 to 2.2) off the kernel before.

The step had a second fault. "Against: no wait of 1.5 us did it" rests on one row, and the same trace has another:

```profile
631.60 5.35 PE L825 MATMUL PS<-ring,KQH 128*64 128x512 f32 x16 [1.66 <-DMA ring<-in_moe_w_up]
```

In before_again even a wait of 1.51 us stands ahead of a half of 5.35 us (1120.61). So the chance of 0.05 for B was not as well founded as it reads; what kept the clock up in the change was not shown by the row that I used.

**Tail: right in kind, too large.** "11.7 us behind the landing" was 11.9, against 12.55 to 12.6 where TensorE is not late: -0.65 per layer, not -0.9, because the second half takes 3.59 us to the start of the sum (737.53 to 741.12) where I had 3.43, and from the transposes to down it is 1.48 (742.94 to 744.42) where I had 1.40. These two also make a pair at the start of the loop 26.9 us, not 26.6, which the full stream hides. With the clock's part the tail gave 2.6 against 1.8.

**Sum.** 5.0 (holes and head) + 1.3 (tail) + 1.3 (clock at the tail) + 0.5 (chance ahead of the loops) = 8.1 between the mean spans of profiles. The timed means differ by 8.1 to 8.9 us in the two later comparisons and by 10.4 in the first, which had four runs of each. In forecast terms: 5.4 became 6.3 by sizes, and the clock is the one that I had at zero.

**The base.** I set the forecast against the median of the three runs, 1314.6. Over 23 runs of one comparison the kernel before had a mean of 1312.4; the change had 1303.5 and 1303.8 over six. The forecast of 1309.2 rested on a base about 2 us high; from 1312.4 the same terms give 1307.0, and the result still lay lower. The "0.5%" that a measurement was said to tell was too coarse as well: the intervals here are 0.1 to 0.2% to either side.

**Rule and trace.** The Trainium skill (TensorE: Matmul & The Clock Gate, HAM oscillation) speaks of waits for a DMA at every tile that send each burst back to half rate. I weighed it against the change. The traces agree with it for the kernel before (2.8 us of waiting, then 5.03, 6.56, 6.61 us), though only at some experts. In down_only the clock falls too, but there the two waits are for VectorE and ScalarE, 1.19 and 0.85 us long. In the change, with its two waits per expert, nothing of the kind is seen: the longest is 1.34 us, and no half and no down product of its five profiles is slow.

**What stays open.** In the nine profiles of the kernel before, head_only, split_only and the kernels with fillers in the old order all 35 waits for weights of 2.5 us and more were followed by a slow half. Of the 69 waits of 1.4 to 2.3 us, 30 were and 39 were not, and nothing here says which. Open too is why the long wait falls on expert 30 in some executions and not in others, and why the timed distance exceeds the sum of the sizes by up to 1 us (2 in the first comparison); four profiles are too few to tell.

## What to carry to other kernels

When a change breaks long waits of TensorE into short ones, ask what the lower clock costs the kernel *before*, at the place where no slack takes it (here the last expert): the lower clock in the profile before is a term of the forecast. When an engine enters a loop behind a stream, its time per step must be under the stream's by enough to catch up: 13.5 against 14.9 us did it within 22 experts, 14.07 almost at the 31st, 14.4 not at all. And a split that earns nothing alone (0.9988 with the head's part, which alone gave 0.9984) can be what makes another edit safe: of "down first" without it 22 us of loss came, with it 9 of gain.

## What the runs showed of the hardware

In down_only, behind two waits of 1.2 and 0.9 us with four 128x128 transposes between them, the down product took 5.35 us instead of 3.65 in 15 of 32 pairs. With one filler product of 128x512 in the first wait (1.13 us at 549.63) of every pair none did, and 25 us came back. The change's own waits, up to 1.34 us with at least half a sum, a half of gate and up or a down product between one stop and the next, stood beside a granted clock of 1.00 over 200 us. In the kernel before every wait for weights of 2.8 us had a gate and up half of 5.0 to 6.7 us behind it, and this cost time only where that half was expert 30's.
